# SBUF tiles on a 256-byte grid from one base, and the loop counts beside the constants

## The reference

```python
for i in range(2):
    z = x @ w_in[i]
    q, k, v, u, g_attn, g_ssm = jnp.split(z, splits, axis=-1)
    a_out = sliding_window_attention(q, k, v, attn_sinks[i], rel_bias)
    s_out = s5_mixer(u, ...)                     # complex diagonal states, gelu, gate y @ w_glu
    merged = (sigmoid(g_attn) * (a_out @ w_branch_attn[i])
              + sigmoid(g_ssm) * (s_out @ w_branch_ssm[i]))
    x = layer_norm(ALPHA * x + merged @ w_out[i], ln1_g[i], ln1_b[i])
    if i % 2 == 0:
        ffn = swiglu(x, ffn_w_gate_up[0], ffn_w_down[0])                        # width 2816
    else:
        ffn = moe_swiglu(x, moe_router[0], moe_w_gate_up[0], moe_w_down[0])     # 8 experts of 3584, top 2
    ple = sigmoid(x @ ple_w_gate[i]) * (p[i] @ ple_w_proj[i])
    x = layer_norm(ALPHA * x + ffn + ple, ln2_g[i], ln2_b[i])
```

## The kernel before

| tile | at (words) | bytes past a multiple of 256, from the base |
|---|---|---|
| ring (six slots of 2048) | 0 | 0 |
| xa, xb, lnp (2048 each; xbh, xIl and hi_norm lie on lnp) | 12288, 14336, 16384 | 0 |
| cst (520: identity, iota, masks, 8 numbers) | 18432 | 0 |
| small (1536: statistics and scalars) | 18952 | 32 |
| pT, xT (xTh and gathered lie on xT), rth, rtl, npass | 20488 to 23176 | 32 |
| bias (wh_spare lies on it) | 23184 | 64 |
| arena, to the end | 25232 | 64 |

## Time and profile before

### The profile page before, as it was taken

One profiled execution on the slowest core, in us unless ns is written; L12 is line 12 of the kernel. 1 busy time (PEld: TensorE's weight loads), 2 busy tenths in 40 slices (PEclk: granted clock), 3 DMA queues, 4 the chain that ended last, 5 costly groups with the idle time before them and its releaser, 6 DMA issues.

```text
span 1611.1 us, 23897 instructions
## 1 busy us (share of the span) xinstructions
PE 1568.9 (97%) x8952; PEld 1332.2 (83%) x8952; DVE 1356.8 (84%) x1316; ACT 975.2 (61%) x887; POOL 160.5 (10%) x151
## 2 busy tenths in 40 slices
PE   7999999999999999999999999999999999999996
PEld 5889789999899978888888888888888888888884
DVE  8976866655688788999998999998999998999998
ACT  3324444434655437776777777677777777767763
POOL 5000139950300000000000000000000000000000
PEclk9999999999999999999999999999999999999998
DMA  7434855554343557999999999999999999999993
GB/s 254 157 106 137 291 193 185 190 193 137 123 139 133 209 216 294 365 364 364 367 364 334 351 370 366 356 366 342 344 367 362 363 372 333 353 371 364 350 366 121
DMA packets 168710, 456.52 MB, mean 283 GB/s; under 512 B 7926, under 2 KB 60183, under 8 KB 168136
## 3 DMA queue, kind: packets, MB, share of 16 engines
q1 hardware_dynamic: 167880, 450.91, 77.2%
q0 software_dynamic: 768, 4.75, 0.8%
HBM read 453.01 MB, written 2.62 MB: 283 GB/s over the span
## 4 chain that ended last, share of the span: by engine, by line
PE 85%; DVE 9%; issue 3%; DMA 2%; ACT 1%; DVEq 0%; SPq 0%; ACTq 0%
PE psum L700 20%; PE psum L701 19%; PE psum L702 19%; PE psum L707 5%; PE psum L708 5%; PE psum L709 5%; PE psum L796 5%; DVE wl L457 2%; PE psum L1154 1%; DMA ring<-in_w_out 1%; PE psum L821 1%; PE psum L769 1%; DVE hid L2144 1%; DMA ring<-in_w_in 1%; DVE small L1750 1%
## 5 line engine op out<-in xcount | busy, mean ns | idle before, releaser
L457 DVE TENSOR_TENSOR wl<-ring,wh 128x2048 fp32r<-128x2048 f32 x269 | 609.6, 2289 | 66.6 <-ACT wh L451 63.0
L451 ACT ACTIVATE wh<-ring 128x2048 fp32r<-128x2048 f32 x307 | 581.4, 1918 | 124.7 <-PE psum L702 76.8
L701 PE MATMUL psum<-wl,xgh 128*128 128x512 f32 x896 | 349.0, 390 | 0.0
L700 PE MATMUL psum<-wh,xgh 128*128 128x512 f32 x704 | 282.0, 401 | 1.0 <-DVE xgl L2128 0.5
L702 PE MATMUL psum<-wh,xgl 128*128 128x512 f32 x704 | 274.9, 390 | 0.0
L701 PEld LDWEIGHTS psum<-wl,xgh 128*128 128x128 f32 x896 | 168.5, 188 | 32.3
L700 PE MATMUL psum<-wh,hidh 128*128 128x512 f32 x440 | 172.7, 393 | 3.7 <-DVE wl L457 2.9
L701 PE MATMUL psum<-wl,hidh 128*128 128x512 f32 x448 | 174.4, 389 | 0.0
L702 PE MATMUL psum<-wh,hidl 128*128 128x512 f32 x440 | 171.4, 389 | 0.0
L457 DVE TENSOR_TENSOR wl<-ring,wh_spare 128x2048 fp32r<-128x2048 f32 x72 | 164.7, 2287 | 3.0 <-ACT wh_spare L451 3.0
L700 PEld LDWEIGHTS psum<-wh,xgh 128*128 128x128 f32 x704 | 132.2, 188 | 33.8 <-DVE wl L457 5.7
(11 more groups left out here) (410 smaller groups left out, 2720.4 us busy)
## 6 DMA issues: line engine op xcount, KB each, us to landing
ring<-in_moe_gu SPq DMA_DIRECT2D x224, 1024.0 KB, 7.0
ring<-in_moe_dn SPq DMA_DIRECT2D x112, 1024.0 KB, 7.1
ring<-in_w_in SPq DMA_DIRECT2D x26, 1024.0 KB, 5.2
ring<-in_w_gu SPq DMA_DIRECT2D x22, 1024.0 KB, 5.0
ring<-in_w_dn SPq DMA_DIRECT2D x11, 1024.0 KB, 4.8
ring<-in_w_out SPq DMA_DIRECT2D x8, 1024.0 KB, 6.4
ring<-in_w_pg SPq DMA_DIRECT2D x8, 1024.0 KB, 4.9
ring<-in_w_ba SPq DMA_DIRECT2D x4, 1024.0 KB, 5.1
```

Source lines behind the costliest of these rows:

```text
L451: eng.activation(parts(u)[0], ring[:, ring_slot(u), :], ACT.Copy).then_inc(hi_ready, 1)
L457: eng.tensor_tensor(lo, ring[:, ring_slot(u), :], hi.bitcast(F32), ALU.subtract).then_inc(lo_ready, 1)
L700: pe.matmul(dst, ah, bh, start=first, stop=False, skip_group_check=True)
L701: pe.matmul(dst, ah, bl, start=False, stop=False, skip_group_check=True)
```

## The change

1. `place` rounds the length of a tile without `at` up to 64 words, 256 bytes, instead of 8 words.
2. `npass` is placed in the words behind the 520 of `cst`, in the 56 that the rounding leaves free there, and no longer takes a place of its own.
3. The arena's length is rounded down to 64 words, in the declaration and in the assertion.

By that small, pT, xT, rth and rtl (with what lies on them) move up by 56 words (224 bytes), and bias and the arena with all its overlays by 48 words (192 bytes). The ring, xa, xb, lnp and cst stay. All engines' instructions and waits are the same, in the same order.

```diff
@@ -100,7 +100,7 @@
             n = int(np.prod(shape[1:]))
             if at is None:
                 at = top[0]
-                top[0] += -(-n // 8) * 8
+                top[0] += -(-n // 64) * 64
                 assert BASE + 4 * top[0] <= END, (name, top[0])
             return nc.alloc_sbuf_tensor_at(name, shape, dt, offset=BASE + 4 * at)
 
@@ -116,7 +116,9 @@
         xbl = place("xbl", [P, NB, D], F32R, at=xb_at)
         lnp_at = top[0]
         lnp = place("lnp", [P, 2, D])
+        cst_at = top[0]
         cst = place("cst", [P, 4 * P + 8])
+        npass = place("npass", [1, 8], I32, at=cst_at + 4 * P + 8)
         small = place("small", [P, 48, 32])
         pT_at = top[0]
         pT = place("pT", [P, 2, SEQ])
@@ -124,13 +126,12 @@
         xT_at = top[0]
         xT = place("xT", [P, KD, SEQ])
         rth, rtl = place("rth", [P, KD, 8], F32R), place("rtl", [P, KD, 8], F32R)
-        npass = place("npass", [1, 8], I32)
 
         bias_at = top[0]
         bias = place("bias", [P, HEADS, SEQ])
         arena_at = top[0]
         ARENA = (END - BASE) // 4 - arena_at
-        arena = place("arena", [P, ARENA // 8 * 8])
+        arena = place("arena", [P, ARENA // 64 * 64])
 
@@ -227,7 +228,7 @@
         raw = cut(4 * ST * SCH, 4, ST)
-        assert at[0] <= ARENA // 8 * 8
+        assert at[0] <= ARENA // 64 * 64
```

## The result

| | before | after |
|---|---|---|
| median of 5 runs | 1616.05 us (1614.34 to 1617.41) | 1623.36 us (1620.84 to 1623.83) |
| span of the profiled execution | 1611.1 us | 1619.0 us |
| mean granted clock over the span | 0.995 | 0.992 |
| PE busy | 1568.9 us | 1576.9 us |

The change makes the kernel **slower by 0.42%**: the ratio is 1.0042, with a 95% interval of 1.0031 to 1.0053, some 7 us. I had forecast no measurable change, 1614.0 us, with a range up to 1620. Two executions far outside all others (3756.57 us of the changed kernel, 5591.73 us of the kernel before) are left out of every ratio.

What follows compares the result with a forecast made beforehand. The prediction took PE's matmul stream, count times start-to-start step, as the bound. It summed 1614.4 + 0 + 0 - 0.5 + 0 + 0 = 1613.9, rounded to 1614.0 us, with a range of 1606 to 1620.

Steps and rivals of the forecast that it cites:

- What bounds the kernel: Whole run: PE's unbroken matmul stream in two thirds of it; time is matmul count times start-to-start step, 0.680 us an expert product.
- Terms 1, 2 and 5: DMAs, VectorE and ScalarE, and the place of npass: each taken as 0 us.
- Term 3: 256-column matmuls in layers 0 and 1 and the branches: -7.5 to +5 us, taken -0.5.
- Term 4: 512-column matmuls in experts, layer 0's down-projection and layer 1's output projection: -1.5 to +27 us, taken 0.
- Rival (B): Experts: the moving operand's own place decides, 0.02 us more a product, 27 us slower, 1641 us; chance 0.08.
- Rival (D): All tiles: the base leaves them 128 bytes off true 256-byte multiples, nothing improves, 1614.4 us; chance 0.60 with the forecast.
- Rival (A): 256-column and mixed ring-arena products: odd places set the slow pace, 1605.4 to 1606.9 us; chance 0.24, wholly or in one layer.
- Rival (C): All 256-column products fall into the shared-place pace, +5.2 us, 1619.6; a low-clock window costs 1.5 us; chance 0.08.
- The rule of the Trainium skill: All SBUF accesses: lines are 16 bytes and only crossings cost, so the change does nothing, 0 rather than -0.5 us.
- The chances: Whole kernel: faster 0.24, same 0.60, slower 0.16, with same meaning within 3.2 us of 1614.4.
- The last sentence of the prediction: PE's steps: no row has a fully aligned moving and stationary pair, which the whole kernel becomes.

Runs made afterwards that it cites:

- e4_probe_starts: The second probe: program replaced by product groups with the kernel's strides, places run from two starts; 256 columns: 0.360 us all at 16 words, 0.340 or 0.353 at 48.
- the first probe: Whole program replaced by groups of 12 products, moving tile's place varied against the stationary's; 256 columns: 0.360 us a product at distance 0, 0.340 at 48 words.
- the fillers: Unread matmuls added where PE waits for LayerNorm: changed kernel 1620.71 us; shorter ones: changed kernel 1617.97, kernel before 1614.06, e7_places 1613.57.
- e2_arena_only: Against the kernel before, only bias and the arena move up by 48 words: 1617.04 us against 1614.41, ratio 1.0015.
- e3_small_only: Against the kernel before, only small, pT, xT, rth and rtl move up by 56 words: ratio 1.0007 (0.9997 to 1.0017).
- e7_places: Against the kernel before, arena on multiples of 256 bytes, moving tiles of 256-column products 8 words off their weights: 1615.31 us, ratio 1.0001.

## Why the prediction was wrong, step by step

- **What bounds the kernel** was right. All of the loss is in PE's steps, and the experts' stream, two thirds of the run, kept its 0.680 us.
- **Terms 1, 2 and 5** (DMAs, VectorE, ScalarE, the counts) came out as forecast: all steps of PE outside the products and the low clock changed by 0.5 us together. VectorE's 128x2048 subtraction takes 2288 ns in the arena and 2287 in the ring, against 2289 and 2288 in the earlier trace rows.
- **Term 3** is the step that failed. The count and the upper end were right: +5 us stood there, 0.360 us a product with "everything on one grid", and it measured +6.0. The value taken, -0.5, was wrong, and by this sentence: "The nearest row to the up-projection after the change is the earlier trace rows". In the earlier trace rows only two of three passes have both operands at the same place; the third has the high part's sister in the ring, 16 words off. After the change all three passes share a place, and the right row would have been one of the pass, not of the product. I had seen that those two passes alone take 0.24 us and used it for an end of the range instead of for the value. The second probe has both cases side by side: 16, 16 / 16, 0 at 0.353 and 16, 16 / 16, 16 at 0.360.
- The end of the range that I had for the 256-column passes was 5.2 us; they took 6.0. The difference lies in the branches and the glu (passes with aTh, aTl, gsh, gsl moving): 160 products and not about 100, up to 0.360 us and not 0.353, +2.3 us where I had priced 1.3. The 560 products of xTh took 3.4 us more, where I had 3.9.
- **Term 4** had the right reading of the earlier trace rows (distance, not the moving tile's own place) and nearly the right price. Its own terms (88 products of 0.007 and 64 of 0.02 us) add up to 1.9 us and not to "some 1.5"; measured were -1.9 in all, -2.5 outside the experts. I then took 0, since "those products lie beside LayerNorm and gating work". In part that was right: PE's idle time ahead of the first transposes grew by 0.37 and 0.29 us. But layer 0's down-projection (0.7 us of the gain) has no such wait.
- **Rival (B)** is refuted: the experts' steps rose by 0.15 ns a pass (0.5 us over 3456 passes), not by 2.4 ns a product or more. **Rival (D)** is refuted by the first probe. **Rival (A)** didn't occur. **Rival (C)** is what happened, in both its halves, and together: I gave it 0.08 and priced 5.2 us for the passes and 1.5 us for one more low-clock stretch. The trace has three more, at +3.5 us together, and the fillers put the clock at 1 to 3 us. The sum had nothing for this: a change of the clock stood in a rival only.
- **The rule of the Trainium skill** that I weighed ("SBUF — State Buffer", the block on "cachelines" under "Door 1", lines of 16 bytes) would have given 0, since no access crosses more lines. The runs say it doesn't settle the matter: with every tile on a multiple of 16 bytes, the product moved between 0.340 and 0.360 us. The same page of the Trainium skill, in "Who interferes with whom" under "SBUF: two separate sides", has PE wait on nobody and gives it two independent read ports, one for the moving operand and one for the weights' load. The probes show a pace that depends on both operands' places; no run here tells where the two meet.
- **The chances.** With terms 3 and 4 at their measured size the sum would have been 1614.4 + 4.1 = 1618.5, above the 3.2 us bound. The measured 1623.36 lies 4.9 us over that: 1.6 since the median of before is 1616.05 with two more runs, and 3.2 that the sum had no term for, left for the clock. Both ends were in the text; the choice between them was the error. The last sentence of the prediction names the gap itself, that no row of before shows a pair with both sides on such a place; it should have moved the value and the chance of slower.

**What stays open.** Why the changed kernel meets more low-clock stretches. All of them begin where PE has just waited for a LayerNorm. Ahead of the first transposes PE idles 1.76 us instead of 1.39 in layer 0 and 1.90 instead of 1.61 in layer 1, with faster 512-column passes just before. These are two lines of before and two of after, with the idle time in brackets:

```profile
197.03 1.09 PE L1003 MATMUL psum<-cst,xb 128*128 128x128 f32 x8 [1.39 <-DVE xb L1758]
...
577.82 1.09 PE L1003 MATMUL psum<-cst,xb 128*128 128x128 f32 x8 [1.61 <-DVE xb L1758]
```

```profile
198.15 1.09 PE L1004 MATMUL psum<-cst,xb 128*128 128x128 f32 x8 [1.76 <-DVE xb L1759]
...
583.48 1.09 PE L1004 MATMUL psum<-cst,xb 128*128 128x128 f32 x8 [1.90 <-DVE xb L1759]
```

e2_arena_only, which has the same faster passes, idles 1.94 and 1.74 us there and has three low stretches to before's two. But the length of the idle time doesn't sort the traces. e3_small_only meets a stretch in layer 1 after only 1.49 us (three in all), and e7_places idles 1.92 and 1.81 us and has a single one (at a mean clock of 0.996, where most of its other runs had 0.993 or 0.994):

```profile
580.34 1.09 PE L1005 MATMUL psum<-cst,xb 128*128 128x128 f32 x8 [1.49 <-DVE xb L1760]
```

```profile
198.49 1.09 PE L1006 MATMUL psum<-cst,xb 128*128 128x128 f32 x8 [1.92 <-DVE xb L1761]
```

So the longer idle time isn't shown as the cause, and these two traces speak against it as the whole of it. What is shown is that the traces with the idle time filled have no such stretch. Which rule turns a distance into stall cycles, and what picks a pace at distances other than 0, is open too: the probes measured it, they don't explain it.

## What to carry to other kernels

Alignment is a relation between tiles that are read at the same time, not a virtue of each: putting all tiles on one grid made every pair of operands alike, and alike was the slow case for the short (256-column) passes and the fast one for the long (512-column) ones. On a kernel bound by PE, read the step from start to start of single passes, by operand pair, before touching addresses; the mean duration of a group hides it. And where a value must be taken between a fast and a slow row, look for the row in which every access has the new relation, not most of them.

## What the runs showed of the hardware

- A float32r pass with a 128x128 stationary operand and the moving operand at the same place modulo 256 bytes steps 120.0 ns at 256 columns and 226.7 ns at 512, at the full clock: 288 and 544 cycles of 2.4 GHz, so 32 cycles over the number of columns at either length. This held with both at 0 and with both at 16 words (e4_probe_starts), and once it had settled.
- At other distances 256-column passes step 113.3 to 120 ns on average, 512-column passes 229 to 233 ns, in patterns that repeat every few passes. At 48 words two starts gave 113.3 and 117.7 ns with the same tiles. 20 and 24 words gave 120 ns on average, as slow as 0.
- Settling takes passes too: right after a 256-column group the first three products of an in-step 512-column stream took 0.70, 0.69 and 0.68 us (e4_probe_starts, all at 0).
- Ahead of the last matmuls, stretches at half the clock (1.2 instead of 2.4 GHz) were 3.4 or 6.8 us long and followed a wait of PE for LayerNorm. Counted by 3.4 us there were five in both traces of the changed kernel, two before, three in e2_arena_only and e3_small_only, one in e7_places, none in the four with fillers.
- The mean granted clock and the time go together. Of 65 runs of the kernel before, the four with 0.992 took 1619.2 to 1620.5 us and the eight with 0.996 took 1613.0 to 1613.9 us, as far apart as the two kernels. The clock isn't the whole spread: with the short fillers and the clock at 0.997 runs still lay 2.7 us apart (1615.99 to 1618.68).
